# Attention scores of pairs 3 to 8 from numbers split into two parts: two whole-array products and a pair of half-array products in place of one half-array pair of full fp32

## The reference, cut to what matters

```
qc = lax.dynamic_slice_in_dim(q, q0, Q_BLOCK, axis=3)
...
s_s = jnp.einsum('bghqd,bgqnkd->bghqnk', qc, k_sel) * scale
...
p_s = _masked_softmax(s_s, mask_s)
o_s = jnp.einsum('bghqnk,bgqnkd->bghqd', p_s, v_sel)
...
s_w = jnp.einsum('bghqd,bgkd->bghqk', qc, kw) * scale
p_w = _masked_softmax(s_w, mask_w)
o_w = jnp.einsum('bghqk,bgkd->bghqd', p_w, vw)
return gc[..., 0:1] * o_c + gc[..., 1:2] * o_s + gc[..., 2:3] * o_w
```

## Time and profile before

| | |
|---|---|
| median of 3 runs | 1704.58 us (1703.75 to 1705.79) |
| profiled execution, its own time | 1703.19 us |
| its span in the trace | 1701.4 us |
| TensorE busy | 1683.7 us, 99% |
| VectorE busy | 1022.6 us, 60% |
| ScalarE busy | 633.8 us, 37% |
| GpSimd busy | 71.0 us, 4% |
| granted TensorE clock | 1.0 throughout |

### The profile page before, as it was taken

One profiled execution on the slowest core, in us unless ns is written; L12 is line 12 of the kernel. 1 busy time (PEld: TensorE's weight loads), 2 busy tenths in 40 slices (PEclk: granted clock), 3 DMA queues, 4 the chain that ended last, 5 costly groups with the idle time before them and its releaser, 6 DMA issues.

```text
span 1701.4 us, 22236 instructions
## 1 busy us (share of the span) xinstructions
PE 1683.7 (99%) x8863; PEld 1330.4 (78%) x8863; DVE 1022.6 (60%) x1661; ACT 633.8 (37%) x999; POOL 71.0 (4%) x92
## 2 busy tenths in 40 slices
PE   8999999999999999999999999999999999999999
PEld 7888888787866778668888888888888866687787
DVE  6666444456978765448444357643445578778784
ACT  5221222231267851333222233222222567556740
POOL 0000000000012310000000000000000000013200
PEclk9999999999999999999999999999999999999999
DMA  7645433246300015123433333324332333301322
GB/s 226 198 158 178 135 100 91 70 120 203 100 2 2 2 44 155 62 87 77 105 93 98 99 105 96 95 73 121 99 99 69 104 109 110 119 26 54 108 75 74
DMA packets 233322, 167.59 MB, mean 99 GB/s; under 512 B 10436, under 2 KB 217532, under 8 KB 233092
## 3 DMA queue, kind: packets, MB, share of 16 engines
q1 hardware_dynamic: 230900, 161.98, 32.8%
q10 hardware_dynamic: 2320, 4.20, 0.7%
HBM read 156.31 MB, written 6.30 MB: 96 GB/s over the span
## 4 chain that ended last, share of the span: by engine, by line
PE 89%; DVE 7%; ACT 2%; issue 1%; DMA 1%; SPq 0%; POOL 0%; DVEq 0%; ACTq 0%
PE bank L1124 24%; PE bank L1126 24%; PE bank L1125 24%; PE turned L1382 3%; PE bank L1370 2%; PE bank L1408 2%; PE bank L1708 2%; PE bank L1577 1%; PE bank L1485 1%; DVE w_lo L1841 1%; PE bank L1691 1%; PE turned L1474 1%; DVE bank L2232 1%; PE turned L1182 0%; DVE T L2149 0%
## 5 line engine op out<-in xcount | busy, mean ns | idle before, releaser
L1124 PE MATMUL bank<-h_hi,w_hi 128*128 128x512 f32 x1192 | 471.1, 395 | 3.0 <-DVE h_lo L1896 1.5
L1125 PE MATMUL bank<-h_lo,w_hi 128*128 128x512 f32 x1192 | 464.7, 390 | 0.0
L1126 PE MATMUL bank<-h_hi,w_lo 128*128 128x512 f32 x1192 | 464.6, 390 | 0.0
L678 ACT ACTIVATE w_hi<-w_raw 128x2048 fp32r<-128x2048 f32 (+2 forms) x132 | 233.2, 1766 | 494.9 <-PE bank L1126 492.4
L1841 DVE TENSOR_TENSOR w_lo<-w_raw,w_hi 128x2048 fp32r<-128x2048 f32 (+3 forms) x133 | 280.0, 2106 | 56.2 <-ACT w_hi L678 53.5
L1124 PEld LDWEIGHTS bank<-h_hi,w_hi 128*128 128x128 f32 x1192 | 223.9, 188 | 60.3 <-issue 12.0
L1126 PEld LDWEIGHTS bank<-h_hi,w_lo 128*128 128x128 f32 x1192 | 223.8, 188 | 46.9
L1125 PEld LDWEIGHTS bank<-h_lo,w_hi 128*128 128x128 f32 x1192 | 223.9, 188 | 46.5 <-issue 1.0
L1124 PE MATMUL bank<-u_hi,w_hi 128*128 128x512 f32 x352 | 137.2, 390 | 0.0
L1125 PE MATMUL bank<-u_lo,w_hi 128*128 128x512 f32 x352 | 137.1, 389 | 0.0
L1126 PE MATMUL bank<-u_hi,w_lo 128*128 128x512 f32 x352 | 137.1, 389 | 0.0
(11 more groups left out here) (446 smaller groups left out, 2307.7 us busy)
## 6 DMA issues: line engine op xcount, KB each, us to landing
w_raw<-in_w_in SPq DMA_DIRECT2D x28, 1024.0 KB, 5.3
w_raw<-in_ffn_w_gate SPq DMA_DIRECT2D x44, 512.0 KB, 3.9
w_raw<-in_ffn_w_up SPq DMA_DIRECT2D x44, 512.0 KB, 5.3
w_raw<-in_ffn_w_down SPq DMA_DIRECT2D x32, 704.0 KB, 4.6
ada_w<-in_ada_w SPq DMA_DIRECT2D x16, 768.0 KB, 6.4
w_raw<-in_w_in SPq DMA_DIRECT2D x19, 512.0 KB, 4.3
w_raw<-in_w_out SPq DMA_DIRECT2D x8, 1024.0 KB, 5.1
w_raw<-in_w_branch_nsa SPq DMA_DIRECT2D x8, 512.0 KB, 5.6
```

The lines of the kernel that those rows point to most:

```text
L678: act.activation(w_hi[s % 2][:, 0:n], w_raw[s % 2][:, 0:n], ACT.Copy).then_inc(s_hi, 1)
L1124: pe.matmul(o, l[0], r[0], start=first, stop=False)
L1125: pe.matmul(o, l[0], r[1], start=False, stop=False)
L1126: return pe.matmul(o, l[1], r[0], start=False, stop=last)
```

## The change

For pairs 2 to 7 both operands of the scores are split. `kz_hi` and `kz_lo` are the parts of all keys, made once, by GpSimd, eight instructions of 128x512 (`key_part`), one behind each `weigh` of units 2 to 9. `q_pair[hp % 2][e]` holds head e's queries twice in 128 partitions: the high part in the head's own half, the low part in the other half. GpSimd makes it by two copies and two subtractions of 64x512 a pair (`query_part`), at units 12, 14 and 16 for pair 2, and for the others behind the last unit of pair hp - 2 and the first two of pair hp - 1. Behind each of the two copies, and each subtraction, GpSimd waits for its end.

The scores of one part are now four products: for each head one over all 128 rows, `q_pair` against `kz_hi`, which sums high x high and low x high at once, and then for each head one over its own 64 rows, high part of the queries against `kz_lo`. All are fp32r. The order within a part is: whole product of head 0, of head 1, half-array product of head 0, of head 1; and then the next part. Low x low is left out. `kz_hi` and `kz_lo` lie in the space of `w_hi[1]` and `w_lo[1]`, free in this stage, and `q_pair` where the last two tiles of `a_hi` and `a_lo` come later.

```diff
@@ -215,6 +215,10 @@
         Pm = [at(f"Pm{i}", [P, 2, S], F32, ARENA + (80 + 4 * i) * KB) for i in range(2)]
         PTm = [at(f"PTm{i}", [P, 2, S], F32, ARENA + (88 + 4 * i) * KB) for i in range(2)]
 
+        kz_hi = at("kz_hi", [P, 2, GROUPS, S], F32R, ARENA - 24 * KB)
+        kz_lo = at("kz_lo", [P, 2, GROUPS, S], F32R, ARENA - 8 * KB)
+        q_pair = [[at(f"q_pair{i}{e}", [P, S], F32R, ARENA + (12 + 2 * i + 16 * e) * KB) for e in range(2)] for i in range(2)]
+
         rq = at("rq", [P, 4, S], F32, N0)
         rk = at("rk", [P, 4, S], F32, N0 + 8 * KB)
         rv = at("rv", [P, NT, 1024], F32, N0 + 16 * KB)
@@ -600,9 +604,44 @@
                     ins = pool.tensor_scalar(p_, p_, mstat[:, u % 2, 8 * i + 6:8 * i + 7], gates[:, t, g0:g0 + 1], ALU.mult, ALU.mult)
                 ins.then_inc(sem("p_ready"), 1)
 
+            def key_part(i):
+
+                b, g = i // 4, i // 2 % 2
+                if i == 0:
+                    pool.wait_ge(acc_free, first_acc["rqk"])
+                if i % 2 == 0:
+                    pool.tensor_copy(kz_hi[:, b, g, :], kz[:, b, g, :]).then_inc(sem("k_high"), 1)
+                else:
+                    pool.wait_ge(sem("k_high"), i // 2 + 1)
+                    pool.tensor_sub(kz_lo[:, b, g, :], kz[:, b, g, :], kz_hi[:, b, g, :]).then_inc(sem("k_split"), 1)
+
+            def query_part(hp, i):
+
+                e = i % 2
+                own, other = slice(64 * e, 64 * e + 64), slice(64 - 64 * e, 128 - 64 * e)
+                q, pair = qT[own, hp, :], q_pair[hp % 2][e]
+                if i < 2:
+                    if i == 0 and hp >= 4:
+                        pool.wait_ge(sem("s_full"), FIRST[hp - 1])
+                    pool.tensor_copy(pair[own, :], q).then_inc(sem("q_high"), 1)
+                    pool.wait_ge(sem("q_high"), 2 * (hp - 2) + e + 1)
+                else:
+                    pool.wait_ge(sem("q_high"), 2 * (hp - 2) + e + 1)
+                    pool.tensor_sub(pair[other, :], q, pair[own, :]).then_inc(sem("q_split"), 1)
+                    pool.wait_ge(sem("q_split"), 2 * (hp - 2) + e + 1)
+
+            QUERY_PARTS = {12: [(2, 0), (2, 1)], 14: [(2, 2)], 16: [(2, 3)]}
+            for hp in range(3, 8):
+                QUERY_PARTS.update({FIRST[hp - 1] - 1: [(hp, 0), (hp, 1)], FIRST[hp - 1]: [(hp, 2)], FIRST[hp - 1] + 1: [(hp, 3)]})
             for u in range(U0):
                 if UNITS[u][0] is not None:
                     weigh(u)
+                if 2 <= u < 10:
+                    key_part(u - 2)
+                if u in QUERY_PARTS:
+                    pool.wait_ge(sem("p_ready"), attended(u))
+                for hp, i in QUERY_PARTS.get(u, []):
+                    query_part(hp, i)
 
             def low_part(h, i):
                 own, other = (slice(64 * e, 64 * e + 64) for e in (h % 2, 1 - h % 2))
@@ -1362,6 +1401,19 @@
                     for m in range(8):
                         ins = pe.matmul(bank[2 * (u % 2)][:, 2 * m * NCP:2 * (m + 1) * NCP], qT[:, m, t * P:(t + 1) * P],
                                         kcz[:, :, m // 4, :], start=True, stop=True)
+                    ins.then_inc(sem("s_full"), 1)
+                    return
+                if hp >= 2:
+                    if u in FIRST:
+                        pe.wait_ge(sem("k_split"), 4)
+                        pe.wait_ge(sem("q_split"), 2 * hp - 2)
+                    for t, b, cols in parts_of(u):
+                        queries, keys = slice(t * P, (t + 1) * P), slice(0, (t + 1) * P)
+                        for e in range(2):
+                            pe.matmul(bank[2 * (u % 2) + e][:, cols], q_pair[hp % 2][e][:, queries], kz_hi[:, b, hp // 4, keys], start=True, stop=False)
+                        for e in range(2):
+                            r = slice(64 * e, 64 * e + 64)
+                            ins = pe.matmul(bank[2 * (u % 2) + e][:, cols], q_pair[hp % 2][e][r, queries], kz_lo[r, b, hp // 4, keys], start=False, stop=True)
                     ins.then_inc(sem("s_full"), 1)
                     return
                 for t, b, cols in parts_of(u):
```

## The result

The changed kernel takes 1720.31 us (median of 4 runs, 1717.24 to 1722.47) against 1704.37 us for the kernel before (4 runs beside it). The ratio is 1.009, with a 95% interval of 1.0078 to 1.0102: slower, as forecast, but 0.8 us above the range of 1707.5 to 1719.5, and 7 above the forecast of 1713.3. The profiled execution has 1717.24 us and a span of 1715.4, 14.0 more than before.

A forecast was written before the change was run, and what follows sets the result against it. TensorE, busy for 99% of the span, was taken as the bound. 8.5 us for its new order, 0.5 for GpSimd, less 0.3 for a covered wait, made 8.7 us more: 1713.3 us, range 1707.5 to 1719.5.

The forecast's parts named there:

- the sum for TensorE: Scores of pairs 2 to 7: array switches and weight loads add 1.41 us a pair, 8.5 us for six pairs.
- the one-part unit: Scores of 512 columns, start to turn: 1.07 us against 1.06 before, so 0.01 us more.
- The 0.3 us taken off for a wait: TensorE's one wait for a weighing, behind a two-part unit of pair 2, covered by longer scores: 0.3 us less.
- Rivals 1 and 2: Scores: 1, no cost for whole/half switches, 1702.0, 8%; 2, narrow or half-array products dearer, 1718.5 or 1720.3, 8%.
- the term for GpSimd: GpSimd's copies and differences fit its idle time; disturbing VectorE at units 12 to 16 adds 0.5 us.
- The eight key instructions fall behind weighings of units 2 to 9, which are further apart: Units 2 to 9: GpSimd's key parts make nothing late on the path; no time was added for them.
- the free end: Units 12 to 16: GpSimd does not disturb VectorE, 0 us; the dear end was 3.8 us.
- The rival at 3.8 us: Units 12 to 16: GpSimd holds VectorE up for 3.8 us in place of 0.5, total 1716.6; chance 6%.

The follow-up runs named there:

- e3: Changed kernel with GpSimd's parts moved to places where VectorE reads banks or works with one SBUF tile: 1714.33 us, ratio 1.0054.
- e4: As e3, but each unit has all whole-array products first, then all half-array ones: 1707.33 us, ratio 1.0018.
- e1: Changed kernel with GpSimd making all parts, but TensorE multiplying scores in fp32 as before, so nothing reads the parts: 1710.38 us, ratio 1.0034.
- e7: As e1, but GpSimd makes only the eight key parts and no query parts: 1708.0 us, ratio 1.0022.
- e6: TensorE's order of e5, with GpSimd's instructions at the changed kernel's places: 1708.35 us, ratio 1.0027.
- e8: The same kernel as e5, run again in more rounds: 1704.78 us, ratio 1.0001.
- e2: Changed kernel with GpSimd filling the parts with zeros in place of copying and subtracting: 1713.56 us, ratio 1.0052.
- e5: As e4, but half-array products first, then whole-array ones: 1702.87 us, ratio 0.9988.

## Why the prediction was right in its direction and wrong in its size

**Right: the sum for TensorE.** By its steps: whole products of both heads and the way out, 0.65 forecast, 577.43 to 578.10 = 0.67; the half-array pair, 0.42 and 0.42. For 256: 0.43 (0.22 + 0.21) and 0.43, then 0.32 and 0.32. For 128: 0.38 and 0.37, then 0.26 and 0.26; for 384: 0.54 and 0.55, then 0.37 and 0.37. The only term off is the one-part unit, 0.03 to 0.04 more in place of 0.01. The 0.3 us taken off for a wait that longer scores cover came true too: no turn behind 520 us waits for GpSimd. A pair is 1.47 more, forecast 1.41, and the whole order 8.46 us by e3, forecast 8.5. Rivals 1 and 2 are out: two-part scores take 1.49 and 1.55, and both whole products of 128 columns together 0.37 with the way out, where two at a quarter of the pace would be 0.42 without it. e4 shows the mechanism: take two switches (each a way out and an entry) out of a two-part unit, and 0.39 and 0.29 us go with them. The Trainium skill (TensorEngine Tiling (Array Packing), Key Properties) has the drain at a change of mode; e4 agrees, at 0.15 to 0.2 us for a way out with its entry.

**Wrong: the term for GpSimd.** The step that failed is "The eight key instructions fall behind weighings of units 2 to 9, which are further apart", and with it "I take 0.5, near the free end, since in the steady round VectorE and GpSimd weigh at the same time and the pace holds". The term measured 5.4 us in e1, of which some 4.6 are the meetings. Two errors are in it.

1. I asked whether a GpSimd instruction fits into GpSimd's own gap. It does: copies take 0.61 to 0.80 us, differences 1.27 to 1.39, and the one turn that waits 0.9 us for GpSimd, at 485.32, waits for a weighing that itself waited for VectorE. The question was what VectorE runs in that gap. Around units 2 to 9 it makes the compressed keys, and TensorE stands behind it. e7 puts 3.5 us on these (2.9 without its fall of the clock), where I had none.
2. Two weighings side by side say little about a difference beside a two-tile instruction. Row and row would have had to match in kind. The rival at 3.8 us, worked out for units 12 to 16 alone, had three meetings of 1.28; there were two, of 0.94 and 0.67, and three where I didn't look.

The Trainium skill (SBUF — State Buffer, Who interferes with whom) says that a VectorE instruction with two inputs in SBUF excludes a GpSimd instruction that reads SBUF, that a VectorE copy can do so too, and that the one issued first keeps the other out until its end. The traces agree: all five began behind the start of a difference, the copy `hrep<-hidT` among them; with one input in a bank, `a_lo<-bank,a_hi` at 528.83 took 0.67 beside a difference, which began at 528.77, and it took 0.67 in the kernel before too, at 522.73, where none runs beside it. The long weighings of the pairs begin by their rows 0.07 to 0.10 us ahead of the copy beside them (541.90 and 541.97), so for these the rows don't show which was first. I had this rule and gave it 6% at a place too narrow.

**Missing: the clock.** No step of the prediction has it. In the profiled execution it is small: ahead of the 17th turn 60.54 us are 55.11 + 4.76 + 0.67, and 0.62 of the 0.67 is what e3 has there from TensorE's order alone. From the 13th turn to the 15th it takes 13.51 us, and e1, which has the same long instructions and the full clock at that place, 12.73. Of these 0.8 us 0.5 are the scores of pair 2's first unit in the new order (e3 takes 11.60 there, the kernel before 11.13), so 0.3 are left for the fall. But the profiled execution is the quickest of the four. The other three have 1718.59, 1722.03 and 1722.47 us at mean clocks of 0.998, 0.996 and 0.996, against its 0.999; e1 has 1708.26 at 1.000 and 1711.99 at 0.997. So 3.7 us between runs of e1 and 5.2 between runs of the changed kernel go along with the clock, and of the median of after, 3.1 above its profile, probably most; that it is the clock is not shown. In which stretches it fell in those runs no trace shows.

The sum as it should have been: 8.5 for the order, 4.6 to 4.8 for five meetings, the rest, 2.6 to 2.8, for the clock and scatter; 15.9 measured between the medians.

What stays open: why the clock falls in one execution and not in the next. With the long instructions (five in after, e1 and e6, three in e7) each of four profiled executions has a fall, at 478.5 to 482.8 or at 514.1 to 517.5; without them, one of five (e8, of e2 to e5 and e8), and not the one of before. (Every execution also ends on 2 to 4 us at half the clock, the one of before too.) In the runs without a profile the kernel before varies too: those with a mean clock of 0.999 have medians 1.5 and 1.7 us above those with 1.000 on the two chips. TensorE's idle time ahead of a fall isn't enough to tell: e5 and e8 have the same, above, and from 474.0 to 478.6 TensorE was busy for 2.67 us in the changed kernel, where no fall followed, and for 2.81 in e1, where one did.

## What to carry to other kernels

Cost an exchange of products on TensorE by the switches between whole and part of the array in program order, as well as by columns: here a way out and an entry were 0.15 to 0.2 us, nearly as much as a whole fp32r product of 512 columns, and grouping the parts of a bank by shape, half-array ones first, gave back what the shorter streams saved (whole ones first, 2.6 us of the 7.8 were left). When work is given to an idle engine, don't ask only whether it fits into that engine's gap, but which instruction of VectorE each of its instructions will lie beside, and whether TensorE is waiting for that one. Where TensorE already has gaps, look at the granted clock of several executions before calling a small gain one.

## What the runs showed of the hardware that I had not expected

- A held-up VectorE instruction costs the rest of GpSimd's instruction and nothing more: in all five meetings it ends 0.14 to 0.15 us ahead of the end of the difference and its own usual time together. The one at 509.48 starts 0.18 behind a difference of 1.27 and takes 1.50 in place of 0.56; the one at 515.72 starts 0.46 behind and takes 1.36 in place of 0.69. For the first, 510.57 + 0.56 - 0.14 = 510.99, seen 510.98.
- Filling a tile on GpSimd isn't free either: in e2 a weighing beside it took 1.02 us, and 0.56 in the kernel before.
- At half the granted clock for 3.4 us the kernel lost only 0.3 to 0.6 us where VectorE set the pace (0.3 at 514, after against e1, less the new order's 0.5; 0.6 at 479, e7 with 11.37 us from the 4th turn to the 7th against 10.79 in after, which has the same long instructions and the full clock there), and 2.7 for 6.8 us in e8.
- A turn costs 0.97 us behind whole-array products and 1.03 behind half-array ones: part of the entry is paid inside the next instruction, where no gap shows.
